# A mixture-of-experts item of 96 token slots instead of 128

## The chip, the core and the metric

One core of a Trainium2 chip runs the whole program. The metric is the device time of one execution in microseconds (us); lower is better. The engines are TensorE (PE; its weight loads, LDWEIGHTS, are listed apart as PEld), VectorE (DVE), ScalarE (ACT), GpSimd (POOL) and the queue engine SyncE (SP).

## The reference, cut to what matters

A decoder trunk of two layers on 256 tokens of 1024 values. Each layer mixes (attention and a recurrence), runs a feed-forward part and adds a gated embedding term. In the second layer the feed-forward part is a mixture of experts:

```
logits = jnp.dot(t, w_router)                        # 256 x 8
top_logit, top_idx = lax.top_k(logits, 2)
top_w = softmax(top_logit)
gate = einsum('tk,tke->te', top_w, one_hot(top_idx, 8))
for e in range(8):
    out = out + gate[:, e:e+1] * ((silu(t @ w_gate[e]) * (t @ w_up[e])) @ w_down[e])
```

Each token goes to two of eight experts, 512 choices in all. An expert's inner width is 3584. All data is 4-byte floating point.

## The kernel before, in words

The work on an expert is an *item*. An item holds up to P = 128 token slots of one expert; if an expert was chosen by more than 128 tokens, a further item is added for the rest (at most OVER of them). The number of items is computed on the chip (`n_items`), and every engine runs a loop over the items.

For an item the 128 tokens are gathered from memory into `xg` (an indirect DMA on POOL, line 529), turned by eight transposes (`turn_tokens`, line 2073) and split into a high and a low part (`uTeh` by ScalarE in `tokens_hi`, line 826; `uTel` by VectorE in `tokens_lo`, line 1419). These are the stationary operands. The weights are the moving operands: they come in chunks of 1 MB (128 x 2048) into a ring `raw` of seven, are split by ScalarE (`whi`, line 599) and VectorE (`wlo`, line 948), and are multiplied in three products (`product`, lines 1601 to 1603: high by high, high by low, low by high), each with 512 moving columns. An item takes 42 chunks in the order `EXP_ORDER`: for each of seven column blocks r of 512 the gate ("g", two halves), the up projection ("u", two halves), and the down projection ("d", two halves) of an earlier block. A gate or up chunk has 4 triples of products, a down chunk 4 as well: 168 triples, 504 products.

The result of a gate block goes through silu (`exs`, line 876), is multiplied with the up block (`exh`, line 1515 on VectorE), is turned by four transposes (`turn`, line 2100), and split again into high (`turn_hi`, line 740, ScalarE) and low (`turn_lo`, line 1500, VectorE); these are the stationary operands of the down products. Each engine works strictly in program order. TensorE issues the four transposes of block r-1 behind the first half of the gate chunk of block r. A transpose has the data as stationary operand and the identity as moving operand. At the end of an item ScalarE copies the 128 x 1024 result out of PSUM (`ysb`, line 840) and POOL scatters its rows (line 553). The last item's result isn't scattered but added by eight products (line 2148).

The slot table: each token's rank within its expert is known from `before` and `ones` products (lines 2052 to 2058). `sel` is a one-hot matrix (token by slot). The first item's tokens are selected by products with it (line 2082, the tokens stationary, `sel` moving; each product is two passes), those of later items by gathers, whose row numbers come from `rows_of_item` (line 2064, `sel` stationary, two moving columns). While item 0 runs, VectorE builds between its splits the table of the items (`table_piece`, one piece per chunk): from chunk OVER_AT = 14 on one overflow column per chunk (`over_item`, lines 1440 to 1443), and behind them one small operation and the list of experts (lines 1458, 1459). Ahead of the loop TensorE also runs transposes that keep it busy (`warm`, line 2031).

Of the kernel before, what the change touches and what calls it, by code (L numbers as in the profile page):

```python
# [41 lines left out]
OVER = (2 * SEQ) // (P + 1)  # L42
# [102 lines left out]
def trunk(nc, x, p, w_in, fox_gate_bias, fox_out_gain, hgrn_lb_logits, hgrn_out_gain, w_out,  # L145
# [3 lines left out]
    with ctx:  # L149
# [94 lines left out]
        exs = [region(512 * i, NC) for i in range(2)]  # L244
        exh = [region(1024 + 512 * i, NC) for i in range(2)]
# [7 lines left out]
        uTeh, uTel = uTh[:, :, 0:P], uTl[:, :, 0:P]  # L253
        exhT = [[hTr[:, i, r * NC:(r + 1) * NC].rearrange("p (c n) -> p c n", c=4) for i in range(2)] for r in range(2)]
# [35 lines left out]
        tprod = small[:, heads_at:heads_at + FIELDS * NE].rearrange("p (a b) -> p a b", a=FIELDS)  # L290
        items = stat(FIELDS * (ITEMS + 1)).rearrange("p (a b) -> p a b", a=FIELDS)
        over, nover, hot = stat(NE), stat(NE), stat(NE)
# [177 lines left out]
        def _(pool):  # L470
# [76 lines left out]
            with pool.Fori(0, last_item) as i:  # L547
# [5 lines left out]
                nc.gpsimd.indirect_dma_start(ybuf, bass.IndirectOffsetOnAxis(ap=put_row, axis=0), ysb, None).then_inc(scattered, 16)  # L553
# [3 lines left out]
        def _(act):  # L557
# [277 lines left out]
            def y_out(i):  # L835
# [3 lines left out]
                for q in range(2):  # L839
                    nc.scalar.activation(ysb[:, q * NC:(q + 1) * NC], bank(5 + q), ACT.Copy).then_inc(y_ready, 1)  # L840
# [27 lines left out]
            def item(i, ahead):  # L868

                for n, (kind, r, hf) in enumerate(EXP_ORDER):  # L870
# [56 lines left out]
        def _(dve):  # L927
# [94 lines left out]
            def rows_to_get(i, b):  # L1022

                dve.wait_ge(row_ps, i + 1)
                link_row(V.tensor_copy(gate_next, bank(b)[:, 1:2]), 8 * i + 1)
                link_row(V.tensor_copy(row_sb, bank(b)[:, 0:1]), 8 * i + 2)
                link_row(V.tensor_scalar(get_row, row_sb, 2.0, -2.0, ALU.max, ALU.add), 8 * i + 3)
                V.tensor_scalar(get_row, get_row, 1, None, ALU.logical_shift_right).then_inc(get_ready, 1)

            def rows_to_put(i):  # L1030

                link_row(V.tensor_scalar(unused, row_sb, 0.0, None, ALU.is_equal), 8 * i + 4)
                link_row(V.tensor_tensor(unused, unused, spare, ALU.mult), 8 * i + 5)
                link_row(V.tensor_copy(tokf[:, 0:1], get_row), 8 * i + 6)
                link_row(V.tensor_copy(gate_of, gate_next), 8 * i + 7)
                dve.wait_ge(scattered, i * 16 + 16)
                V.scalar_tensor_tensor(put_row, row_sb, -2.0, unused, ALU.add, ALU.add).then_inc(put_ready, 1)
# [6 lines left out]
            def choose_slots():  # L1044

                for t in range(TT):
                    V.tensor_scalar(sel[:, t, :], iota[:, :], iitem[:, t:t + 1], None, ALU.is_equal).then_inc(sel_ready, 1)
# [360 lines left out]
            for t in range(TT):  # L1408
                V.tensor_scalar(sel[:, t, :], iota[:, :], table[:, t, 0:1], None, ALU.is_equal).then_inc(sel_ready, 1)
            link(V.tensor_scalar(over, bank(RANKS)[:, 2 * NE:3 * NE], float(P), None, ALU.is_gt))  # L1410
            link(V.tensor_tensor_scan(nover, ones[:, 0:NE], over, 0.0, ALU.mult, ALU.add))
            for k in range(2):
                V.tensor_scalar(item_expert[:, ITEMS + k:ITEMS + k + 1], nover[:, NE - 1:NE], float(NE - k), None, ALU.add).then_inc(count_ready, 1)
            V.tensor_copy(iitem[:, 0:4], table[:, 0:4, 0]).then_inc(first_rows, 1)

            def tokens_lo(i, q):

                dve.wait_ge(euh_ready, i * 2 + (q + 1))
                V.tensor_tensor(uTel[:, 4 * q:4 * q + 4, :], bank(TOKENS[q], 4, P), uTeh[:, 4 * q:4 * q + 4, :].bitcast(F32),
# [18 lines left out]
            def over_item(n):  # L1438

                link(V.tensor_scalar(hot, nover, float(n + 1), None, ALU.is_equal))  # L1440
                link(V.tensor_tensor(hot, hot, over, ALU.mult))
                link(V.tensor_tensor(tprod, table, hot.unsqueeze(1).to_broadcast([P, FIELDS, NE]), ALU.mult))
                link(V.tensor_reduce(items[:, :, NE + n], tprod, AX, ALU.add))

            def table_piece(n):
# [11 lines left out]
                elif n == OVER_AT + OVER:  # L1457
                    link(V.tensor_scalar(items[:, 0:2, NE:ITEMS], items[:, 0:2, NE:ITEMS], -float(P), None, ALU.add))
# [14 lines left out]
            def last_slots():  # L1473

                link(V.tensor_scalar(tokf[:, 1:2], tokf[:, 0:1], -float(P), None, ALU.add))
                for t in range(TT):
                    V.tensor_scalar(slot_of[:, t, :], iota[:, :], tokf[:, t:t + 1], gate_of, ALU.is_equal, ALU.mult).then_inc(slot_ready, 1)
# [735 lines left out]
```

## Time and profile before

| | |
|---|---|
| median of 3 runs | 1541.87 us (1541.39 to 1544.29) |
| profiled execution, span from first to last instruction | 1540.0 us, 21230 instructions |
| what lies around the span (median less span) | 1.87 us |
| busy: PE, PEld, DVE, ACT, POOL | 1518.3, 1281.1, 1231.6, 996.5, 53.9 us |
| mean granted clock of TensorE | 0.997 of 2.4 GHz |
| DMA | 453.38 MB, mean 294 GB/s |
| loads of each of the three expert weights | x112, 1024 KB each (8 items x 14) |

The profile is of one execution; its own device time isn't listed apart from the span, so a change is worked out on the span and then put on the median. Matmuls are pipelined: the recorded time of one is from its start to its modelled end and is longer than the distance to the next one's start. A group like "x8" in a timeline has the time from the first start to the last end.

### The profile page before, as it was taken

The page shows a single profiled execution, that of the slowest core. Times are in us where ns is not written, and L with a number is a line of the kernel's source. Part 1 is how long each engine was busy: PE and PEld are TensorE (multiplying, and loading weights), DVE is VectorE, ACT ScalarE, POOL GpSimd, SP SyncE. Part 2 cuts the span into 40 slices and gives each one's busy share as a digit, 9 for nine tenths or more (in the row PEclk, how much of TensorE's full clock was granted, in tenths as well). Part 3 has the DMA queues.
Part 4 walks back from the last instruction along what each step waited for, and adds up shares of the span by engine and source line. Part 5 has one row for each costly group of instructions (what it writes and reads, how often), then busy time and mean ns, then how long its engine had stood idle before and what let it go on. Part 6 is the DMA issues. An engine that isn't in the chain of part 4 may idle for free.

```text
span 1540.0 us, 21230 instructions
## 1 busy us (share of the span) xinstructions
PE 1518.3 (99%) x7976; PEld 1281.1 (83%) x7976; DVE 1231.6 (80%) x1100; ACT 996.5 (65%) x852; POOL 53.9 (4%) x76
## 2 busy tenths in 40 slices
PE   7999999999999999999999999999999999999998
PEld 6988888888998888888888888888888888888876
DVE  5877545557786679988889889888988889898887
ACT  6544444346725367787787687687787787777666
POOL 5000000000000000000000000000000000000000
PEclk9999999999999999999999999999999999999999
DMA  9432765545533479999999999999999999999990
GB/s 304 138 110 83 256 202 186 188 168 183 165 110 123 172 278 363 383 372 377 378 374 386 378 371 387 373 374 388 374 375 391 370 373 393 369 375 390 373 391 30
DMA packets 206787, 453.38 MB, mean 294 GB/s; under 512 B 12488, under 2 KB 31504, under 8 KB 206480
## 3 DMA queue, kind: packets, MB, share of 16 engines
q1 hardware_dynamic: 200368, 439.22, 79.2%
q0 software_dynamic: 2880, 10.49, 1.8%
q10 hardware_dynamic: 3488, 2.99, 0.6%
q8 instruction: 33, 0.54, 0.1%
q14 instruction: 18, 0.15, 0.0%
HBM read 444.80 MB, written 7.86 MB: 294 GB/s over the span
## 4 chain that ended last, share of the span: by engine, by line
PE 94%; DVE 3%; ACT 1%; DMA 1%; issue 1%; SPq 0%; DVEq 0%; ACTq 0%
PE bank L1601 28%; PE bank L1603 28%; PE bank L1602 28%; PE bank L1692 2%; PE bank L2100 2%; DVE wlo L948 1%; PE bank L1799 1%; PE bank L1752 1%; PE bank L1596 1%; ACT whi L599 0%; DMA raw<-in_w_exp_gate_dram 0%; DMA raw<-in_w_in_dram 0%; PE bank L1766 0%; PE bank L2073 0%; PE bank L1701 0%
## 5 line engine op out<-in xcount | busy, mean ns | idle before, releaser
L948 DVE TENSOR_TENSOR wlo<-raw,whi 128x2048 fp32r<-128x2048 f32 x415 | 937.1, 2288 | 144.5 <-ACT whi L599 92.8
L599 ACT ACTIVATE whi<-raw 128x2048 fp32r<-128x2048 f32 x341 | 638.1, 1911 | 45.5 <-DMA raw<-in_w_exp_down_dram 22.9
L1601 PE MATMUL bank<-whi,uTh 128*128 128x512 f32 (+1 forms) x1304 | 512.0, 393 | 0.9 <-DVE uTl L1014 0.5
L1603 PE MATMUL bank<-whi,uTl 128*128 128x512 f32 (+1 forms) x1304 | 503.8, 386 | 0.0
L1602 PE MATMUL bank<-wlo,uTh 128*128 128x512 f32 (+1 forms) x1304 | 502.8, 386 | 0.0
L1603 PEld LDWEIGHTS bank<-whi,uTl 128*128 128x128 f32 x1304 | 244.9, 188 | 50.6
L1601 PEld LDWEIGHTS bank<-whi,uTh 128*128 128x128 f32 x1304 | 245.1, 188 | 49.1 <-DVE uTl L1014 0.7
L1602 PEld LDWEIGHTS bank<-wlo,uTh 128*128 128x128 f32 x1304 | 245.3, 188 | 46.8
L1601 PE MATMUL bank<-whi,hTr 128*128 128x512 f32 x528 | 207.3, 393 | 0.4 <-DVE hTr L1500 0.4
L1603 PE MATMUL bank<-whi,hTr 128*128 128x512 f32 x528 | 205.7, 390 | 0.0
L1602 PE MATMUL bank<-wlo,hTr 128*128 128x512 f32 x528 | 205.5, 389 | 0.0
L591 ACT ACTIVATE whi<-raw 128x2048 fp32r<-128x2048 f32 x74 | 138.8, 1912 | 0.9 <-DMA raw<-in_w_in_dram 0.8
L740 ACT ACTIVATE hTr<-bank 128x512 fp32r<-128x512 f32 x56 | 33.6, 599 | 153.2 <-PE bank L2100 153.2
L1603 PEld LDWEIGHTS bank<-whi,hTr 128*128 128x128 f32 x528 | 99.1, 188 | 20.9
L1601 PEld LDWEIGHTS bank<-whi,hTr 128*128 128x128 f32 x528 | 99.2, 188 | 20.7 <-issue 0.8
L1602 PEld LDWEIGHTS bank<-wlo,hTr 128*128 128x128 f32 x528 | 99.2, 188 | 20.1
L1601 PE MATMUL bank<-uTh,whi 128*128 128x256 f32 x256 | 74.1, 290 | 0.0
L1602 PE MATMUL bank<-uTl,whi 128*128 128x256 f32 x256 | 72.4, 283 | 0.0
L1603 PE MATMUL bank<-uTh,wlo 128*128 128x256 f32 x256 | 72.4, 283 | 0.0
L783 ACT ACTIVATE hTr<-bank 128x512 fp32r<-128x512 f32 x10 | 5.4, 595 | 74.2 <-PE bank L1955 74.2
L649 ACT ACTIVATE work<-bank 128x512 f32<-128x512 f32 x24 | 14.3, 597 | 57.0 <-PE bank L1603 54.1
L1601 PEld LDWEIGHTS bank<-uTh,whi 128*128 128x128 f32 x256 | 49.1, 192 | 1.2
(294 smaller groups left out, 1086.8 us busy)
## 6 DMA issues: line engine op xcount, KB each, us to landing
raw<-in_w_exp_gate_dram SPq DMA_DIRECT2D x112, 1024.0 KB, 6.0
raw<-in_w_exp_up_dram SPq DMA_DIRECT2D x112, 1024.0 KB, 6.2
raw<-in_w_exp_down_dram SPq DMA_DIRECT2D x112, 1024.0 KB, 6.1
raw<-in_w_in_dram SPq DMA_DIRECT2D x28, 1024.0 KB, 5.4
raw<-in_w_ffn_gate_dram SPq DMA_DIRECT2D x11, 1024.0 KB, 5.3
raw<-in_w_ffn_up_dram SPq DMA_DIRECT2D x11, 1024.0 KB, 5.1
raw<-in_w_ffn_down_dram SPq DMA_DIRECT2D x11, 1024.0 KB, 4.8
raw<-in_w_out_dram SPq DMA_DIRECT2D x8, 1024.0 KB, 5.1
```

Source lines behind the costliest of these rows:

```text
L591: nc.scalar.activation(whi[:, n % SPLIT, :], raw[:, n % RAW, :], ACT.Copy).then_inc(hi_a, 1)
L599: nc.scalar.activation(whi[:, s % SPLIT, :], raw[:, s % RAW, :], ACT.Copy).then_inc(hi_a, 1)
L740: nc.scalar.activation(exhT[r % 2][0], bank(4, 4, P), ACT.Copy).then_inc(exT_hi, 1)
L948: return V.tensor_tensor(wlo[:, n % RAW, :], raw[:, n % RAW, :], whi[:, n % SPLIT, :].bitcast(F32), ALU.subtract).then_inc(lo_ready, 1)
L1596: last = T.transpose(bank(4 + 2 * t + q, 4, P)[:, c, :], un[:, t, (4 * q + c) * P:(4 * q + c + 1) * P], ident[:, :])
L1601: T.matmul(o, sth, mvh, start=start, stop=False)
L1602: T.matmul(o, sth, mvl, start=False, stop=False)
L1603: return T.matmul(o, stl, mvh, start=False, stop=stop)
L1692: last = T.matmul(b[:, t * NP + hp, :], keyT[r, hp, t * P:(t + 1) * P], later, start=True, stop=True)
L1752: last = T.matmul(bank(FOX_BANK[t])[:, hd * HD:(hd + 1) * HD], probsT[u][:, i * nk + kt, :], fv[:, kt, hd * HD:(hd + 1) * HD], start=kt == ...
L1799: last = T.matmul(bank(b[t]), st[:, hf * HALF + k, t * P:(t + 1) * P], mv[:, k, :], start=start and k == 0, stop=stop and k == HALF - 1)
L2100: last = T.transpose(bank(4, 4, P)[:, c, :], exh[r % 2][:, c * P:(c + 1) * P], ident[:, :])
```

## The change

CAP = 96 replaces P = 128 as the number of slots of an item. `uTeh`, `uTel` and `exhT` are 96 columns wide, so that the stationary operands of the products, the PSUM rows that they write, `exs`, `exh` and `ysb` have 96 rows. Transposes read 96 rows and have a 96 x 96 identity. Gather and scatter move 96 rows. An expert of more than 96 tokens gets a second item and one of more than 192 a third; so at most five items are added instead of three (OVER), `over` has two comparisons (96, 192) side by side, and `over_item` works on 2 x 8 columns. The moving operands of the products keep 512 columns, and the loads of weights stay as they are.

```diff
-OVER = (2 * SEQ) // (P + 1)
+CAP = 96
+MORE = (SEQ - 1) // CAP
+OVER = (2 * SEQ) // (CAP + 1)
...
-        exs = [region(512 * i, NC) for i in range(2)]
-        exh = [region(1024 + 512 * i, NC) for i in range(2)]
+        exs = [region(512 * i, NC)[0:CAP, :] for i in range(2)]
+        exh = [region(1024 + 512 * i, NC)[0:CAP, :] for i in range(2)]
...
-        uTeh, uTel = uTh[:, :, 0:P], uTl[:, :, 0:P]
-        exhT = [[hTr[:, i, r * NC:(r + 1) * NC].rearrange("p (c n) -> p c n", c=4) for i in range(2)] for r in range(2)]
+        uTeh, uTel = uTh[:, :, 0:CAP], uTl[:, :, 0:CAP]
+        exhT = [[hTr[:, i, r * NC:r * NC + 4 * CAP].rearrange("p (c n) -> p c n", c=4) for i in range(2)] for r in range(2)]
...
-                nc.gpsimd.indirect_dma_start(xg, None, tok, bass.IndirectOffsetOnAxis(ap=get_row, axis=0)).then_inc(xg_in, 16)
+                nc.gpsimd.indirect_dma_start(xg[0:CAP, :], None, tok, bass.IndirectOffsetOnAxis(ap=get_row[0:CAP, :], axis=0)).then_inc(xg_in, 16)
...
-                nc.scalar.activation(exhT[r % 2][0], bank(4, 4, P), ACT.Copy).then_inc(exT_hi, 1)
+                nc.scalar.activation(exhT[r % 2][0], bank(4, 4, CAP), ACT.Copy).then_inc(exT_hi, 1)
...
-                nc.scalar.activation(uTeh[:, 4 * q:4 * q + 4, :], bank(TOKENS[q], 4, P), ACT.Copy).then_inc(euh_ready, 1)
+                nc.scalar.activation(uTeh[:, 4 * q:4 * q + 4, :], bank(TOKENS[q], 4, CAP), ACT.Copy).then_inc(euh_ready, 1)
...
-                V.tensor_scalar(sel[:, t, :], iota[:, :], table[:, t, 0:1], None, ALU.is_equal).then_inc(sel_ready, 1)
-            link(V.tensor_scalar(over, bank(RANKS)[:, 2 * NE:3 * NE], float(P), None, ALU.is_gt))
-            link(V.tensor_tensor_scan(nover, ones[:, 0:NE], over, 0.0, ALU.mult, ALU.add))
+                V.tensor_scalar(sel[:, t, 0:CAP], iota[:, 0:CAP], table[:, t, 0:1], None, ALU.is_equal).then_inc(sel_ready, 1)
+            for k in range(MORE):
+                V.tensor_scalar(over[:, k * NE:(k + 1) * NE], bank(RANKS)[:, 2 * NE:3 * NE], float((k + 1) * CAP), None, ALU.is_gt).then_inc(dchain, 1)
...
+            link(V.tensor_tensor_scan(nover, ones[:, 0:MORE * NE], over, 0.0, ALU.mult, ALU.add))
...
-                link(V.tensor_scalar(hot, nover, float(n + 1), None, ALU.is_equal))
-                link(V.tensor_tensor(hot, hot, over, ALU.mult))
-                link(V.tensor_tensor(tprod, table, hot.unsqueeze(1).to_broadcast([P, FIELDS, NE]), ALU.mult))
-                link(V.tensor_reduce(items[:, :, NE + n], tprod, AX, ALU.add))
+                link(V.scalar_tensor_tensor(hot, nover, float(n + 1), over, ALU.is_equal, ALU.mult))
+                link(V.tensor_reduce(above[:, n:n + 1], hot[:, NE:MORE * NE], AX, ALU.add))
+                hots = hot.rearrange("p (m b) -> p m b", m=MORE).unsqueeze(1).to_broadcast([P, FIELDS, MORE, NE])
+                link(V.tensor_tensor(tprod, table.unsqueeze(2).to_broadcast([P, FIELDS, MORE, NE]), hots, ALU.mult))
+                link(V.tensor_reduce(items[:, :, NE + n], tprod.rearrange("p a m b -> p a (m b)"), AX, ALU.add))
...
-                V.tensor_tensor(exh[r % 2], bank(2 + r % 2), exs[r % 2], ALU.mult).then_inc(exh_ready, 1)
+                V.tensor_tensor(exh[r % 2], bank(2 + r % 2)[0:CAP, :], exs[r % 2], ALU.mult).then_inc(exh_ready, 1)
...
-                        last = T.transpose(bank(TOKENS[q], 4, P)[:, c, :], xg[:, k * P:(k + 1) * P], ident[:, :])
+                        last = T.transpose(bank(TOKENS[q], 4, CAP)[:, c, :], xg[0:CAP, k * P:(k + 1) * P], ident[0:CAP, 0:CAP])
...
-                        last = T.matmul(bank(TOKENS[q], 4, P)[:, c, :], un[:, t, k * P:(k + 1) * P], sel[:, t, :], start=t == 0, stop=t == TT - 1)
+                        last = T.matmul(bank(TOKENS[q], 4, CAP)[:, c, :], un[:, t, k * P:(k + 1) * P], sel[:, t, 0:CAP], start=t == 0, stop=t == TT - 1)
...
-                        last = T.transpose(bank(4, 4, P)[:, c, :], exh[r % 2][:, c * P:(c + 1) * P], ident[:, :])
+                        last = T.transpose(bank(4, 4, CAP)[:, c, :], exh[r % 2][:, c * P:(c + 1) * P], ident[0:CAP, 0:CAP])
...
-                            last = product(bank(5 + q), exhT[r % 2][0][:, cc, :], exhT[r % 2][1][:, cc, :], wh[:, c, s], wl[:, c, s],
+                            last = product(bank(5 + q)[0:CAP, :], exhT[r % 2][0][:, cc, :], exhT[r % 2][1][:, cc, :], wh[:, c, s], wl[:, c, s],
...
-                            last = product(bank((0 if kind == "g" else 2) + r % 2), uTeh[:, kk, :], uTel[:, kk, :],
+                            last = product(bank((0 if kind == "g" else 2) + r % 2)[0:CAP, :], uTeh[:, kk, :], uTel[:, kk, :],
```

## Rows read from the trace of the kernel before

**Rows 1.** Page, part 1: busy time, share of the span, instructions.
```profile
PE 1518.3 (99%) x7976; PEld 1281.1 (83%) x7976; DVE 1231.6 (80%) x1100; ACT 996.5 (65%) x852; POOL 53.9 (4%) x76
```

**Rows 2.** Page, part 4: the chain that ended last, by engine.
```profile
PE 94%; DVE 3%; ACT 1%; DMA 1%; issue 1%; SPq 0%; DVEq 0%; ACTq 0%
```

**Rows 3.** Windows: length; busy PE, PEld, DVE, ACT, POOL; granted clock, DMA share, GB/s.
```profile
536.00:537.00 1.00, 1.00 (x6) 1.00 (x5) 0.90 (x6) 0.00 (x0) 0.00 (x0) 0.50 0.00 0
...
700.00:800.00 100.00, 100.00 (x459) 82.79 (x458) 88.63 (x57) 76.11 (x53) 4.08 (x4) 1.00 1.02 374
```

**Rows 4.** The gather's line: ns min/median/max, first and last start.
```profile
L529 POOL DMA_INDIRECT work<-tok,small x8: 961/962/1017, 625.9 to 1459.9; - x8
```

**Rows 5.** Groups by line and shape: busy us, mean ns, idle before, by whom.
```profile
L1601 PE MATMUL bank<-whi,hTr 128*128 128x512 f32 x528 | 207.3, 393 | 0.4 <-DVE hTr L1500 0.4
...
L1500 DVE TENSOR_TENSOR hTr<-bank,hTr 128x512 fp32r<-128x512 f32 x56 | 38.5, 688 | 9.1 <-ACT hTr L740 9.0
...
L2100 PE MATMUL bank<-ident,work 128*128 128x128 f32 x224 | 33.6, 272 | 0.8 <-DVE work L1515 0.8
```

**Rows 6.** Timeline of TensorE in the expert loop: start us, us.
```profile
900.65 0.39 PE L1601 MATMUL bank<-whi,hTr 128*128 128x512 f32 x1
900.65 0.19 PEld L1602 LDWEIGHTS bank<-wlo,hTr 128*128 128x128 f32 x1
...
903.37 0.39 PE L1601 MATMUL bank<-whi,uTh 128*128 128x512 f32 x1
```

**Rows 7.** Timeline in layer 0, 256 moving columns, then 64-row operands.
```profile
62.49 0.28 PE L1602 MATMUL bank<-uTl,whi 128*128 128x256 f32 x1
...
62.61 0.28 PE L1603 MATMUL bank<-uTh,wlo 128*128 128x256 f32 x1
62.82 0.97 PEld L1692 LDWEIGHTS bank<-work 64*128 64x128 f32 x16
```

**Rows 8.** Timeline: eight transposes of an item's tokens.
```profile
652.20 1.03 PE L2073 MATMUL bank<-ident,work 128*128 128x128 f32 x8
```

**Rows 9.** Single lines of TensorE: duration ns min/median/max, first and last start.
```profile
L2040 PEld LDWEIGHTS bank<-wr,work x32: 186/192/192, 523.6 to 532.1; 128*128 128x128 f32 x32
L2040 PE MATMUL bank<-wr,work x32: 175/256/277, 523.7 to 532.2; 128*128 128x8 f32 x32
...
L2073 PEld LDWEIGHTS bank<-ident,work x64: 138/140/141, 652.0 to 1486.9; 128*128 128x128 f32 x64
...
L2148 PE MATMUL bank<-work x8: 592/592/697, 1499.5 to 1502.6; 128*128 128x512 f32 x8
```

**Rows 10.** Timeline ahead of the expert loop.
```profile
523.70 1.85 PE L2040 MATMUL bank<-wr,work 128*128 128x8 f32 x16
...
537.44 5.20 PE L2082 MATMUL bank<-work,un 128*128 128x128 f32 x32
540.89 0.60 ACT L826 ACTIVATE uTh<-bank 128x512 fp32r<-128x512 f32 x1 [5.62 <-PE bank L2082]
```

**Rows 11.** Timeline of VectorE in item 0, chunks 14 to 21.
```profile
590.27 0.17 DVE L1440 TENSOR_SCALAR small<-small 128x8 f32<-128x8 f32 x1
...
590.67 0.22 DVE L1442 TENSOR_TENSOR small<-small 128x56 f32<-128x56 f32 x1
...
591.17 0.69 DVE L1515 TENSOR_TENSOR work<-bank,work 128x512 f32<-128x512 f32 x1
...
594.88 0.69 DVE L1500 TENSOR_TENSOR hTr<-bank,hTr 128x512 fp32r<-128x512 f32 x1
...
598.78 2.29 DVE L948 TENSOR_TENSOR wlo<-raw,whi 128x2048 fp32r<-128x2048 f32 x1 [0.23 <-DVE small L1443]
...
607.88 0.68 DVE L1515 TENSOR_TENSOR work<-bank,work 128x512 f32<-128x512 f32 x1
```

**Rows 12.** Timeline of TensorE in the same stretch.
```profile
595.70 0.49 PE L1601 MATMUL bank<-whi,hTr 128*128 128x512 f32 x1 [0.37 <-DVE hTr L1500]
...
609.43 0.60 PE L2100 MATMUL bank<-ident,work 128*128 128x128 f32 x4
```

More of the change, by code:

```diff
@@ L289, in trunk @@
         table = stat(FIELDS * NE).rearrange("p (a b) -> p a b", a=FIELDS)
-        tprod = small[:, heads_at:heads_at + FIELDS * NE].rearrange("p (a b) -> p a b", a=FIELDS)
+        tprod = small[:, heads_at:heads_at + FIELDS * MORE * NE].rearrange("p (a m b) -> p a m b", a=FIELDS, m=MORE)
         items = stat(FIELDS * (ITEMS + 1)).rearrange("p (a b) -> p a b", a=FIELDS)
-        over, nover, hot = stat(NE), stat(NE), stat(NE)
+        over, nover, hot, above = stat(MORE * NE), stat(MORE * NE), stat(MORE * NE), stat(OVER)
         iitem = stat(6)
@@ L552, in _ @@
                 nc.gpsimd.tensor_tensor(idle, spare, spare, ALU.add).then_inc(pool_turn, 1)
-                nc.gpsimd.indirect_dma_start(ybuf, bass.IndirectOffsetOnAxis(ap=put_row, axis=0), ysb, None).then_inc(scattered, 16)
+                nc.gpsimd.indirect_dma_start(ybuf, bass.IndirectOffsetOnAxis(ap=put_row[0:CAP, :], axis=0), ysb[0:CAP, :], None).then_inc(scattered, 16)
             fetch(n_items, n_items * 2)
@@ L1024, in rows_to_get @@
                 dve.wait_ge(row_ps, i + 1)
[L1025 to L1028, printed above, removed]
+                link_row(V.tensor_copy(gate_next[0:CAP, :], bank(b)[0:CAP, 1:2]), 8 * i + 1)
+                link_row(V.tensor_copy(row_sb[0:CAP, :], bank(b)[0:CAP, 0:1]), 8 * i + 2)
+                link_row(V.tensor_scalar(get_row[0:CAP, :], row_sb[0:CAP, :], 2.0, -2.0, ALU.max, ALU.add), 8 * i + 3)
+                V.tensor_scalar(get_row[0:CAP, :], get_row[0:CAP, :], 1, None, ALU.logical_shift_right).then_inc(get_ready, 1)
             def rows_to_put(i):
[L1032 to L1035, printed above, removed]
+                link_row(V.tensor_scalar(unused[0:CAP, :], row_sb[0:CAP, :], 0.0, None, ALU.is_equal), 8 * i + 4)
+                link_row(V.tensor_tensor(unused[0:CAP, :], unused[0:CAP, :], spare[0:CAP, :], ALU.mult), 8 * i + 5)
+                link_row(V.tensor_copy(tokf[0:CAP, 0:1], get_row[0:CAP, :]), 8 * i + 6)
+                link_row(V.tensor_copy(gate_of[0:CAP, :], gate_next[0:CAP, :]), 8 * i + 7)
                 dve.wait_ge(scattered, i * 16 + 16)
-                V.scalar_tensor_tensor(put_row, row_sb, -2.0, unused, ALU.add, ALU.add).then_inc(put_ready, 1)
+                V.scalar_tensor_tensor(put_row[0:CAP, :], row_sb[0:CAP, :], -2.0, unused[0:CAP, :], ALU.add, ALU.add).then_inc(put_ready, 1)
             def link_row(ins, n):
@@ L1046, in choose_slots @@
                 for t in range(TT):
-                    V.tensor_scalar(sel[:, t, :], iota[:, :], iitem[:, t:t + 1], None, ALU.is_equal).then_inc(sel_ready, 1)
+                    V.tensor_scalar(sel[:, t, 0:CAP], iota[:, 0:CAP], iitem[:, t:t + 1], None, ALU.is_equal).then_inc(sel_ready, 1)
             def choose(t):
@@ L1408, in _ @@
             for t in range(TT):
[L1409 to L1411 removed]
+                V.tensor_scalar(sel[:, t, 0:CAP], iota[:, 0:CAP], table[:, t, 0:1], None, ALU.is_equal).then_inc(sel_ready, 1)
+            for k in range(MORE):
+                V.tensor_scalar(over[:, k * NE:(k + 1) * NE], bank(RANKS)[:, 2 * NE:3 * NE], float((k + 1) * CAP), None, ALU.is_gt).then_inc(dchain, 1)
+            chain[0] += MORE
+            dve.wait_ge(dchain, chain[0])
+            link(V.tensor_tensor_scan(nover, ones[:, 0:MORE * NE], over, 0.0, ALU.mult, ALU.add))
             for k in range(2):
[L1413 removed]
+                V.tensor_scalar(item_expert[:, ITEMS + k:ITEMS + k + 1], nover[:, MORE * NE - 1:MORE * NE], float(NE - k), None, ALU.add).then_inc(count_ready, 1)
             V.tensor_copy(iitem[:, 0:4], table[:, 0:4, 0]).then_inc(first_rows, 1)
@@ L1457, in table_piece @@
                 elif n == OVER_AT + OVER:
-                    link(V.tensor_scalar(items[:, 0:2, NE:ITEMS], items[:, 0:2, NE:ITEMS], -float(P), None, ALU.add))
+                    ranks_over = items[:, 0:2, NE:ITEMS]
+                    link(V.scalar_tensor_tensor(ranks_over, above.unsqueeze(1).to_broadcast([P, 2, OVER]), -float(CAP), ranks_over, ALU.mult, ALU.add))
+                    link(V.tensor_scalar(ranks_over, ranks_over, -float(CAP), None, ALU.add))
                     V.tensor_copy(item_expert[:, 0:ITEMS], items[:, FIELDS - 1, 0:ITEMS]).then_inc(table_ready, 1)
@@ L1473, in last_slots @@
             def last_slots():
-                link(V.tensor_scalar(tokf[:, 1:2], tokf[:, 0:1], -float(P), None, ALU.add))
+                link(V.tensor_scalar(tokf[0:CAP, 1:2], tokf[0:CAP, 0:1], -float(P), None, ALU.add))
                 for t in range(TT):
-                    V.tensor_scalar(slot_of[:, t, :], iota[:, :], tokf[:, t:t + 1], gate_of, ALU.is_equal, ALU.mult).then_inc(slot_ready, 1)
+                    V.tensor_scalar(slot_of[0:CAP, t, :], iota[0:CAP, :], tokf[0:CAP, t:t + 1], gate_of[0:CAP, :], ALU.is_equal, ALU.mult).then_inc(slot_ready, 1)
             def add_last(t):
@@ L2063, in rows_of_item @@
                 for t in range(TT):
-                    last = T.matmul(bank(b)[:, 0:2], sel[:, t, :], iitem[:, 2 + t:5 + t:2], start=t == 0, stop=t == TT - 1)
+                    last = T.matmul(bank(b)[0:CAP, 0:2], sel[:, t, 0:CAP], iitem[:, 2 + t:5 + t:2], start=t == 0, stop=t == TT - 1)
                 last.then_inc(row_ps, 1)
@@ L2147, in _ @@
                         pe.wait_ge(y_ready, n_items * 2 + (1 + q))
-                    T.matmul(bank(LAST_BANK[t][q]), slot_of[:, t, :], ysb[:, q * NC:(q + 1) * NC], start=True, stop=True).then_inc(last_y, 1)
+                    T.matmul(bank(LAST_BANK[t][q]), slot_of[0:CAP, t, :], ysb[0:CAP, q * NC:(q + 1) * NC], start=True, stop=True).then_inc(last_y, 1)
             embed(1, tail_in(0), 0)
```

10 lines of the change are left out of this document (5 added, 5 removed).

## The prediction

> **What bounds the kernel now.** I read the page first, then the windows, then single stretches of the timeline. TensorE is busy for 99% of the span [rows 1], and the chain that ended last is 94% TensorE [rows 2]. The view by windows repeats this for the expert loop: in 700 to 800 us TensorE is busy for 100.00 of 100 us at the full granted clock (2.4 GHz), VectorE for 88.63, ScalarE for 76.11 [rows 3]. The gather for the next item starts first at 625.9 and last at 1459.9 us, eight times [rows 4], so an item takes (1459.9 - 625.9)/7 = 119.1 us and eight of them some 950 of the 1540 us.
>
> Busy time says nothing of pace, so I looked at starts. Two products of line 1601 stand twelve products apart at 900.65 and 903.37 [rows 6]: one starts every 2.72/12 = 0.2267 us, though each is recorded as 0.39 us. With 256 moving columns the starts are 0.120 apart [rows 7]. So a moving column costs (226.7 - 120)/256 = 0.417 ns and 13.3 ns remain per product, with either width. The weight load (0.19 us) starts with the product before it and lies under it. An item has 168 triples, 504 products: 504 x 0.2267 = 114.3 us. Its 36 transposes start (1.03 - 0.272)/7 = 0.108 us apart [rows 5, 8]: 3.9 us. Together 118.2 of 119.1. The item's time is therefore set by moving columns and transposes; what lies on other engines is free as long as TensorE does not wait.
>
> **The change part by part.** The reference's router, evaluated on its inputs, gives the eight experts 66, 65, 55, 64, 45, 82, 67 and 68 of the 512 choices. None passes 96, so no overflow item is added and there stay eight items. If one were, it would cost 119.1 us.
>
> (1) *The 4032 expert products.* The moving side stays 512 columns; only the stationary side goes from 128 to 96 columns. What could answer to that is the remainder of 13.3 ns. No row has a stationary side under 128 columns. If the remainder were in proportion to the width it would fall by 3.3 ns, 13.5 us in all; if it were to vanish, 54 us; if it grew by as much as the first, +13.5. I take 0: transposes swap 128 columns of weights just as often and show only 108 - 107 = 1 to 2 ns (below), so the 13.3 ns do not come from swapping a wide operand. The shorter weight load is hidden under 0.2267 us of the product before it; it has 0.04 us to grow before it shows.
>
> (2) *The transposes.* The data is the stationary operand and keeps 128 columns; the identity is the moving one and goes from 128 to 96. A moving column of this 4-byte kind costs (592 - 272)/384 = 0.833 ns (512 columns in line 2148, 128 in line 2100) [rows 5, 9], so 128 cost 106.7 ns: the whole interval of 108 but 1 to 2 ns. Then 96 cost 80, and an interval falls by 26.7 ns, provided that the weight load isn't the limit. Bounds: 0 if it is, 26.7 if not. The router's products (line 2040) tell what the limit of a load is: with only 8 moving columns they start (1.85 - 0.256)/15 = 0.106 us apart [rows 9, 10], so a load that is recorded as 192 ns takes the array for 0.106. A transpose's load is recorded as 140 ns, 52 shorter [rows 9]; if the fixed part is the same it takes the array for 0.054. That is under 80, and I take the gain. It holds between transposes only: the product behind the last one needs a load of the long kind (0.106), as now. Seven groups of four give 3 intervals each, the group of eight gives 7: 28 x 26.7 = 0.75 us per item, x8 = -6.0 us.
>
> The Trainium skill ("TensorE: Matmul & The Clock Gate", LDWEIGHTS) has a load take its column count over 1.2 GHz, which is 107 ns for 128 columns, transposes not excepted. By it every transpose would stay at 107 and this term would be 0. The interval of line 2040 agrees with it, the 140 ns of the transposes' loads speak against it.
>
> (3) *The row products (line 2064)*: four per item, 2 moving columns, so bound by their load; 96 columns instead of 128 at 0.106/128 per column take 26 ns less each. 4 x 0.026 x 8 = -0.8 us; bounds 0 and -0.8. I take -0.8.
>
> (4) *Ahead of the loop*: the 32 passes that select the first item's tokens (line 2082) get 96 moving columns. Until 540.89 they start (540.89 - 537.44)/16 = 0.216 us apart, twice 0.106, at the lower clock (granted 0.50, 1.2 GHz) [rows 3, 10]; their load keeps 128 columns, so I take 0 (bound: 16 x 0.053 = -0.85). Behind them lie one ScalarE and one VectorE operation on 384 instead of 512 columns: 0.60 and 0.69 us for 512 [rows 5, 10], some 0.1 us less each: -0.2. The two comparisons and the longer scan on VectorE come before 540 us, while TensorE is in line 2082: nothing.
>
> (5) *The table in item 0.* VectorE now makes five overflow columns and not three, between the weight splits. One costs 591.17 - 590.27 = 0.90 us now [rows 11]. With 112 elements for 56 in the product and the reduction (0.22 against 0.17 for 8 elements: 0.05 per 48, so 0.06 more each) and 16 for 8 elsewhere I take 1.08. VectorE is already late there: line 1515 at 591.17 and line 1500 at 594.88 follow without a gap, and TensorE idles before the product behind (0.37) [rows 11, 12]. The first two columns lie in this stretch: 2 x 0.18 - 0.13 (line 1500 is shorter) = +0.23. From there to line 1515 at 607.88 come one longer column, two new ones and one more small operation: 0.18 + 2.16 + 0.2 = 2.54. VectorE has 0.23 idle (598.78), and line 1515 ends at 608.56 while TensorE wants it at 609.43 [rows 12]: 0.8 of slack after the hand-over. 2.54 - 0.23 - 0.8 = +1.5. Later gaps absorb the rest. Together +1.7; bounds +0.2 (ScalarE, not VectorE, was late) and +2.9 (all that is added shows).
>
> (6) *Hidden*: lines 740 and 1500 lose some 0.1 us in each of 56 turns, silu and the gate product keep their 512 columns, the gathers and scatters move a quarter fewer rows. TensorE waited 0.4 us for line 1500 in the whole kernel [rows 5] and for no gather, so this gives nothing; without that cover it would be some 0.2 us per turn, 56 times, -11.
>
> Sum: 0 - 6.0 - 0.8 - 0.2 + 1.7 = -5.3 us on a span of 1540.0. The span plus 1.87 us is the median of the runs shown; the time is thus 1541.87 - 5.3 = 1536.6 us (-0.34%).
>
> **The rivals.**
> *Loads bind the transposes* (the change does not do what it could): term 2 falls away. 1541.87 - 1.0 + 1.7 = 1542.6, no change. For it: 0.108 is also next to the 0.106 of a load. Against: the record of 140 ns.
> *The remainder follows the width*: 4032 x 3.3 ns = 13.5 us more gain, 1523; the same upwards, 1550. For it: nothing in the trace fixes the remainder. Against: it is the same for 256 and 512 moving columns and absent in transposes.
> *A drain at every change of shape* (slower). When the stationary rows go from 128 to 64, the load isn't pulled ahead: it starts at 62.82, 0.21 after the product at 62.61, where the next load otherwise starts with the product, and that product's interval is 0.12 [rows 7]; the next start comes 0.2 us late. After the change transposes are 96 rows by 128 columns and products 128 by 96, and they alternate 16 times per item. 16 x 8 x 0.2 = +25.6, so 1562. It decides (over +3.1 us net) from (3.1 + 5.3)/128 = 0.066 us per switch. Against: transposes and products of one shape are all that the loop shows.
> The Trainium skill ("TensorEngine Tiling (Array Packing)", Key Properties and Column Tiling) says that a change of tiling mode drains the engine, with modes for up to 64 rows or columns; 96 would be the full mode, and by it nothing drains. The switch at 62.61 agrees; no run here shows 96.
> *An overflow item*: 1661, excluded by the counts.
>
> **How the numbers follow.** Forecast 0.52; loads bind 0.18; remainder smaller 0.12, larger 0.09; drain 0.08; overflow 0.01. What a measurement of this kernel tells from no change is about 0.2%, 3.1 us. The forecast's own range is 1534 (the item-0 term hidden but for 0.2, and a little less in term 2) to 1540 (half of term 2, all of term 5); 0.07 of its 0.52 lie within 0.2%. Faster: 0.45 + 0.12 = 0.57. Same: 0.07 + 0.16. Slower: 0.09 + 0.08 + 0.01 + 0.02. The range goes from 1523 (remainder in proportion) to 1547 (loads bind, all of term 5, and half a nanosecond more per product).
>
> **What the profile after would show.** Starts of expert products still 0.2267 apart; the eight transposes of line 2073 in 0.83 instead of 1.03 us and their duration 245 instead of 272 ns; an item 0.8 us shorter, 118.3; in item 0 a wait of TensorE for line 1515 of some 1.5 us; DMA issues still x112 per weight. The prediction is wrong if the product interval moves by a nanosecond (4 us), if the load of a transpose shows as the limit, or if a load is no longer pulled ahead at a switch.

## The result, and the profile after

The changed kernel takes 1546.93 us (median of 6 runs, 1544.68 to 1549.13), the kernel before on the same chip 1542.32 us (6 runs, 1540.97 to 1544.53). The ratio is 1.0027 [1.0017, 1.0037]: 4.6 us slower, where 1536.6 us (5.3 us faster) was forecast. Line numbers have moved on by two to eight: the products are now lines 1609 to 1611, the transposes 2108 (block) and 2081 (tokens), the gather 531, VectorE's gate product 1523 and its low half 1508.

The page of the kernel after, busy time, chain and one DMA line:

```profile
PE 1524.4 (99%) x7976; PEld 1170.2 (76%) x7976; DVE 1223.1 (79%) x1110; ACT 987.0 (64%) x852; POOL 74.2 (5%) x76
...
PE 94%; DVE 3%; DMA 1%; ACT 1%; issue 0%; SPq 0%; DVEq 0%; ACTq 0%
...
raw<-in_w_exp_gate_dram SPq DMA_DIRECT2D x112, 1024.0 KB, 5.6
```

Beside [rows 1, 2] all is as announced but one thing: weight loads, VectorE and ScalarE have less to do, no item was added (x112), TensorE is still 94% of the chain, and yet its busy time rose by 6.1 us with the same 7976 instructions. The window in the loop, with the columns of [rows 3]:

```profile
700.00:800.00 100.00, 100.00 (x457) 70.66 (x456) 86.38 (x56) 75.91 (x54) 6.14 (x4) 1.00 1.02 372
```

TensorE is as full as before, at the same full granted clock, and starts 457 instructions where it started 459. It isn't waiting more; its instructions start further apart. The timeline of TensorE, for [rows 6]:

```profile
902.12 0.39 PE L1609 MATMUL bank<-whi,hTr 128*96 128x512 f32 x1
902.12 0.16 PEld L1610 LDWEIGHTS bank<-wlo,hTr 128*96 128x96 f32 x1
...
904.89 0.39 PE L1609 MATMUL bank<-whi,hTr 128*96 128x512 f32 x1
```

These starts too are twelve products apart: 2.77/12 = 0.2308 us, against 0.2267. The load fell from 0.19 to 0.16 us and still starts with the product ahead of it. The recorded duration shows next to none of this (0.39 us in both, 389 and 392 ns in the median of lone products further down): only starts do. A timeline rounds to 10 ns, so I also took the mean distance of neighbouring products in 680 to 1480 us: 227.3 ns over 3268 pairs before, 230.3 ns over 3252 after, +3.0.

The transposes, for [rows 4, 8, 9], views by timeline and by source line:

```profile
656.73 0.82 PE L2081 MATMUL bank<-ident,work 96*128 96x96 f32 x8
...
L2081 PEld LDWEIGHTS bank<-ident,work x64: 138/140/143, 656.5 to 1494.4; 96*128 96x128 f32 x64
L2081 PE MATMUL bank<-ident,work x64: 243/246/248, 656.7 to 1494.5; 96*128 96x96 f32 x64
...
L531 POOL DMA_INDIRECT work<-tok,small x8: 970/3290/3304, 632.8 to 1467.3; - x8
```

Eight in 0.82 us of 246 ns each: starts (0.82 - 0.246)/7 = 0.082 apart, as forecast (0.83 in all, 245 each). The loads of this line give the time of an item, (1494.4 - 656.5)/7 = 119.70 us, against (1486.9 - 652.0)/7 = 119.27 before [rows 9]: +0.43 where -0.8 was expected.

Around one turn of a block in the loop, kernel after:

```profile
716.20 0.40 PE L1611 MATMUL bank<-whi,uTl 128*96 128x512 f32 x1
716.44 0.49 PE L2108 MATMUL bank<-ident,work 96*128 96x96 f32 x4
716.72 0.45 PE L1609 MATMUL bank<-whi,uTh 128*96 128x512 f32 x1
717.01 0.39 PE L1610 MATMUL bank<-wlo,uTh 128*96 128x512 f32 x1
```

From the first transpose to the second product 0.57 us pass; before it was 0.68 (712.50 to 713.18 in its trace), and over the 47 turns in 680 to 1480 us the means are 0.565 and 0.669. For one item: 504 x 3.0 ns = +1.51; seven turns at -0.104 = -0.73; the tokens' turn -0.21; the row products -0.12. Together +0.45, where +0.43 was measured; the measured one times eight is +3.4 us.

Item 0, where VectorE makes five columns and not three (kernel after, VectorE then TensorE):

```profile
593.27 0.17 DVE L1445 SCALAR_TENSOR_TENSOR small<-small 128x16 f32<-128x16 f32 x1
594.29 0.69 DVE L1523 TENSOR_TENSOR work<-bank,work 96x512 f32<-96x512 f32 x1
...
613.15 0.68 DVE L1523 TENSOR_TENSOR work<-bank,work 96x512 f32<-96x512 f32 x1
```

```profile
612.47 0.40 PE L1611 MATMUL bank<-whi,uTl 128*96 128x512 f32 x1
613.89 0.55 PE L2108 MATMUL bank<-ident,work 96*128 96x96 f32 x4 [1.02 <-DVE work L1523]
```

A column costs 594.29 - 593.27 = 1.02 us (0.90 before, 1.08 forecast). TensorE starts the transposes of block 3 at 613.89, 1.42 us after the product ahead instead of 0.23: a stall of 1.19 us.

So +3.4 for eight items, +1.2 for item 0, and -0.3 from line 2063 to the first expert product (9.99 us against 10.27): +4.3 of the +4.6. The profiled execution was the longest of its kernel (span 1547.3, +7.3 on before). Of the rest of that, 1.7 us lie ahead of the first product of line 1700 (64.6 us after the start, before 62.8; two experiments built on the changed kernel have 64.2 and 62.5, and one built on the kernel before has 64.0) and 1.4 us between lines 1916 and 2063 ahead of the loop, where the clock stood at half for longer: at 0.50 from 533.3 to 543.5 us, against 533.7 to 540.5 in before. The same stretch took 10.5 us in before and in all seven experiments on whole kernels, so neither belongs to the change.

### The profile page after: what moved, and what is told of

It is laid out like the page before. It is cut to its first block, busy times and chain, and to the rows that moved or that the text cites. A ratio compares the mean times of both kernels' runs of the same rounds, so it can differ in the third digit from the quotient of the medians.

```text
span 1547.3 us, 21242 instructions
## 1 busy us (share of the span) xinstructions
PE 1524.4 (99%) x7976; PEld 1170.2 (76%) x7976; DVE 1223.1 (79%) x1110; ACT 987.0 (64%) x852; POOL 74.2 (5%) x76
## 4 chain that ended last, share of the span: by engine, by line
PE 94%; DVE 3%; DMA 1%; ACT 1%; issue 0%; SPq 0%; DVEq 0%; ACTq 0%
PE bank L1609 28%; PE bank L1611 28%; PE bank L1610 28%; PE bank L1700 2%; DVE wlo L950 2%; PE bank L2108 1%; PE bank L1807 1%; PE bank L1760 1%; DMA raw<-in_w_exp_up_dram 1%; PE bank L1604 1%; DMA raw<-in_w_in_dram 0%; PE bank L1774 0%; PE bank L1709 0%; PE bank L1734 0%; PE bank L2081 0%
## 5 line engine op out<-in xcount | busy, mean ns | idle before, releaser
L1609 PE MATMUL bank<-whi,uTh 128*96 128x512 f32 (+2 forms) x1304 | 511.8, 392 | 0.8 <-DVE uTl L1016 0.6
L1611 PE MATMUL bank<-whi,uTl 128*96 128x512 f32 (+2 forms) x1304 | 505.2, 387 | 0.0
L1610 PE MATMUL bank<-wlo,uTh 128*96 128x512 f32 (+2 forms) x1304 | 504.7, 387 | 0.0
L1611 PEld LDWEIGHTS bank<-whi,uTl 128*96 128x96 f32 (+1 forms) x1304 | 221.2, 170 | 76.2
L1609 PEld LDWEIGHTS bank<-whi,uTh 128*96 128x96 f32 (+1 forms) x1304 | 221.4, 170 | 73.4 <-DVE uTl L1016 0.7
L1610 PEld LDWEIGHTS bank<-wlo,uTh 128*96 128x96 f32 (+1 forms) x1304 | 221.6, 170 | 70.8
L1609 PE MATMUL bank<-whi,hTr 128*96 128x512 f32 (+1 forms) x528 | 208.5, 395 | 0.5 <-DVE hTr L1508 0.5
L1611 PE MATMUL bank<-whi,hTr 128*96 128x512 f32 (+1 forms) x528 | 207.1, 392 | 0.0
L1610 PE MATMUL bank<-wlo,hTr 128*96 128x512 f32 (+1 forms) x528 | 206.6, 391 | 0.0
L1611 PEld LDWEIGHTS bank<-whi,hTr 128*96 128x96 f32 (+1 forms) x528 | 87.2, 165 | 34.6
L1609 PEld LDWEIGHTS bank<-whi,hTr 128*96 128x96 f32 (+1 forms) x528 | 87.2, 165 | 33.6 <-issue 0.9
L1610 PEld LDWEIGHTS bank<-wlo,hTr 128*96 128x96 f32 (+1 forms) x528 | 87.4, 166 | 33.1
```

The lines of the kernel that those rows point to most:

```text
L1609: T.matmul(o, sth, mvh, start=start, stop=False)
L1610: T.matmul(o, sth, mvl, start=False, stop=False)
L1611: return T.matmul(o, stl, mvh, start=False, stop=stop)
```

## The experiments

Each ratio is to the kernel before on the same chip. Product intervals are the mean over neighbouring products in 680 to 1480 us. "After" or "before" says which kernel an edit starts from.

### Products 128 wide again, all else as after

```diff
-        uTeh, uTel = uTh[:, :, 0:CAP], uTl[:, :, 0:CAP]
+        uTeh, uTel = uTh[:, :, 0:P], uTl[:, :, 0:P]
-        exhT = [[hTr[:, i, r * NC:r * NC + 4 * CAP].rearrange(...) for i in range(2)] for r in range(2)]
+        exhT = [[hTr[:, i, r * NC:(r + 1) * NC].rearrange(...) for i in range(2)] for r in range(2)]
...
-   last = T.transpose(bank(4, 4, CAP)[:, c, :], exh[r % 2][...], ident[0:CAP, 0:CAP])
+   last = T.transpose(bank(4, 4, P)[:, c, 0:CAP], exh[r % 2][...], ident[0:CAP, 0:CAP])
...
-   last = product(bank(5 + q)[0:CAP, :], exhT[r % 2][0][:, cc, :], ...)
+   last = product(bank(5 + q), exhT[r % 2][0][:, cc, :], ...)
```

> The changed kernel, but the expert products have 128 stationary columns again (gate, up and down; 128 output rows); transposes, gathers, the slot table and the item count stay as changed. The columns from 96 on hold whatever lay there, no slot uses them. The two ScalarE and VectorE splits of a turn are 512 wide again. Theory A (the product itself gets slower with 96 stationary columns): starts back to 227.0 ns apart, 4032 x 3.2 = 13 us less than the changed kernel, so some 1534 us, 0.5% under the kernel before. Theory B (something around the products, the narrower loads of transposes or the other engines' new rhythm, stretches them): starts stay at 230 ns and the time at 1546.

Measured: 1536.74 us (1535.3 to 1539.72), ratio 0.9971 [0.996, 0.9981]; product interval 227.3 ns.

```profile
900.26 0.39 PE L1609 MATMUL bank<-whi,hTr 128*128 128x512 f32 x1
...
902.98 0.39 PE L1609 MATMUL bank<-whi,hTr 128*128 128x512 f32 x1
...
L2081 PEld LDWEIGHTS bank<-ident,work x64: 138/140/143, 654.3 to 1483.2; 96*128 96x128 f32 x64
```

The starts, twelve products apart, are 2.72 us from each other, as in [rows 6]. An item takes (1483.2 - 654.3)/7 = 118.41 us, 0.86 less than before. With the products' width back, the rest of the change gains what the forecast had for it. The whole miss is in the products.

### Before, with only the products 96 wide

```diff
-   last = product(bank(5 + q), exhT[r % 2][0][:, cc, :], exhT[r % 2][1][:, cc, :], ...)
+   last = product(bank(5 + q)[0:96, :], exhT[r % 2][0][:, cc, 0:96], exhT[r % 2][1][:, cc, 0:96], ...)
...
-   last = product(bank(...), uTeh[:, kk, :], uTel[:, kk, :], ...)
+   last = product(bank(...)[0:96, :], uTeh[:, kk, 0:96], uTel[:, kk, 0:96], ...)
```

> The kernel before, with one edit: the expert products use 96 of the 128 stationary columns and write 96 output rows; all else is 128 wide. Slots from 96 on are not computed (none is filled). Theory A: starts 230.3 ns apart, +13 us, 1555 us, slower than both kernels. Theory B: 227 ns and 1542 us.

Measured: 1551.58 us (1551.52 to 1554.0), ratio 1.0071 [1.0057, 1.0085]; interval 230.0 ns. The timeline of TensorE:

```profile
713.04 0.60 PE L2100 MATMUL bank<-ident,work 128*128 128x128 f32 x4
713.40 0.48 PE L1601 MATMUL bank<-whi,uTh 128*96 128x512 f32 x1
713.72 0.39 PE L1602 MATMUL bank<-wlo,uTh 128*96 128x512 f32 x1
...
905.90 0.39 PE L1601 MATMUL bank<-whi,uTh 128*96 128x512 f32 x1
...
908.66 0.39 PE L1601 MATMUL bank<-whi,uTh 128*96 128x512 f32 x1
```

Twelve products in 2.76 us, and the turn of a block still 0.68 us. 4032 x 2.7 ns = 10.9 us; by the ratio it is 1542 x 0.0071 = 10.9. The data behind the operands, their places and all other work were those of before: the width alone does it.

### After, with three overflow columns

```diff
-OVER = (2 * SEQ) // (CAP + 1)
+OVER = (2 * SEQ) // (P + 1)
```

> The changed kernel with three overflow columns in the table instead of five (a table for at most three extra items, as before; no input here needs any). Takes two of the pieces of 0.99 us out of VectorE's item 0. If the wait of TensorE in item 0 (1.19 us at the turn of block 3) comes from them, it vanishes and the time falls by some 1.2 us (1545.7), else nothing changes.

Measured: 1543.41 us (1542.87 to 1546.2), ratio 1.0015 [1.0006, 1.0024]. From the first block's transposes to item 1's tokens pass 94.5 us against 95.7 after: 1.2 us, the stall seen above. The intervals of the ratios just overlap, but the trace names the place.

### Products by themselves at several widths

No part of the reference is left: rows of 60 products of one width, behind each other on TensorE.

```diff
+for j in range(REPS):
+    T.matmul(b[0:M, 0:N], st[0:K, j % 16, c0:c0 + M], mv[0:K, j % 4, 0:N], ...)
```

> A kernel of its own, nothing of the reference: rows of 60 back-to-back products on resident data, with no DMA and no other engine at work, for stationary widths of 128, 120, 112, 104, 97, 96, 88, 80, 65, 64 and 32 columns, 96 columns from column 32 on, 96 rows by 128 and by 96, with 256 moving columns, and in the two-pass 4-byte form. Theory A: 227.0 ns at 128 and 230.3 at 96 columns here too. If the interval depends on a multiple of 32 or on the load's length, the other widths show which. Theory B: no difference between widths, and perhaps 215 ns throughout, since no other engine reads memory.

Each row gives (time - duration of one)/59:

```profile
24.15 14.22 PE L77 MATMUL bank<-mv,st 128*120 128x512 f32 x60
...
205.58 7.45 PE L77 MATMUL bank<-mv,st 128*128 128x256 f32 x60
...
212.89 7.20 PE L77 MATMUL bank<-mv,st 128*96 128x256 f32 x60
...
323.15 13.89 PE L77 MATMUL bank<-mv,st 128*128 128x512 f32 x60
...
336.90 14.03 PE L77 MATMUL bank<-mv,st 128*96 128x512 f32 x60
```

With 512 moving columns: 128 wide 228.8 ns, 120 234.3, 112 230.1, 104 230.0, 97 234.1, 96 231.1, 88 234.2, 80 233.8, 65 235.1, 64 230.5, 32 231.8. With 256 the sign turns round: 121.4 for 128, 117.3 for 96. So the cost shows without whi, wlo, VectorE or any DMA beside it, isn't in proportion to the width, and is no property of 96: of these widths, none is faster than 128. With 96 rows instead of 128 the intervals are the same (228.5 and 231.2). The first distance of a row is longer than the rest (0.31 us behind a product 128 wide); without it the means are 227.4 ns for 128 and 230.0 for 96, just those of the kernels. As two-pass products, the widths take 429.8 and 429.6 ns for each pass (120 records for 60 products).

### Before, with the products 120 wide

The edit is that of the second experiment with 0:120 for 0:96.

> The kernel before with the expert products 120 columns wide instead of 128 (slots from 120 on are not computed; none is filled). The row of lone products gave starts 234.3 ns apart at 120 columns against 228.8 at 128. If the width alone sets the interval in the kernel too: starts 5 ns further apart than before, some 232.5 ns, and 1562 us. If 96 is special, or the interval is in proportion to the columns left out: under 1 ns more, 1545 us at most.

Measured: 1565.38 us (2 runs, 1564.29 to 1566.46), ratio 1.0148 [1.0125, 1.017]; interval 233.3 ns.

```profile
903.13 0.40 PE L1601 MATMUL bank<-whi,hTr 128*120 128x512 f32 x1
...
905.94 0.40 PE L1601 MATMUL bank<-whi,hTr 128*120 128x512 f32 x1
```

A cut of eight columns costs 23 us: 4032 x 6.0 ns = 24. The lone products' order of 128, 96 and 120 holds in the kernel.

### Lone products with fewer moving columns, and moved in their tile

No part of the reference is left here either. Rows of 100 products; M columns from column `so` of the stationary tile, N from `mo` of the moving one.

> Lone products again, rows of 100: 128 and 96 stationary columns at 512, 480, 448, 384, 320 and 256 moving columns, then with the first stationary column at 8, 16, 32, 64 and the first moving column at 8, 32. If a narrow operand costs something fixed per product, 96 stays 2 to 3 ns above 128 at every moving width. If it is how the load's reads fall into the running product (a collision in memory), the difference depends on the moving width and on the addresses, and may change sign (the first such kernel had 117.3 for 96 and 121.4 for 128 at 256 moving columns).

```profile
275.63 23.49 PE L78 MATMUL bank<-mv,st 128*128 128x512 f32 x100
...
298.98 22.94 PE L78 MATMUL bank<-mv,st 128*128 128x512 f32 x100
...
344.80 23.05 PE L78 MATMUL bank<-mv,st 128*96 128x512 f32 x100
...
507.52 22.92 PE L78 MATMUL bank<-mv,st 128*128 128x512 f32 x100
...
530.30 23.23 PE L78 MATMUL bank<-mv,st 128*96 128x512 f32 x100
```

The last two are plain: 227.6 and 230.7 ns. The first is 128 wide from column 32: 233.3; the second from column 64: 227.8; the third 96 wide from column 16: 228.9. A move of the operand, with the same shape, is worth up to 6.5 ns (column 16: 234.1), more than the step from 128 to 96 columns. Between 480 and 320 moving columns neither width wins by more than 1.3 ns (217.7 and 219.0; 147.4 and 147.2), except at 448: 207.4 and 203.3.

### The move in the kernel: before from column 32, after from column 16

```diff
-        uTeh, uTel = uTh[:, :, 0:P], uTl[:, :, 0:P]
+        uTeh, uTel = uTh[:, :, 32:32 + P], uTl[:, :, 32:32 + P]
```
```diff
-        uTeh, uTel = uTh[:, :, 0:CAP], uTl[:, :, 0:CAP]
+        uTeh, uTel = uTh[:, :, 16:16 + CAP], uTl[:, :, 16:16 + CAP]
```

> The kernel before with one edit: the tokens' stationary operands (gate and up products, 2688 of the 4032) lie 32 columns (128 bytes) further on; width 128, nothing else changes. Theory A (the number of stationary columns sets the interval): 227 ns and 1542 us, no change. Theory C (the addresses that a load reads while the product before it streams set it; width is one way to change them): the lone products gave 233.3 ns for this offset, so 6 ns x 2688 = +16 us, 1558 us, and down products unchanged at 227.

> The changed kernel with the tokens' stationary operands 16 columns (64 bytes) further on, still 96 wide. Theory A: 1546 us, no change. Theory C: the lone products gave 228.9 instead of 230.7 ns for this offset at 96 columns, so -1.8 x 2688 = -5 us, 1541 us.

Measured, before moved: 1555.39 us (1554.67 to 1556.27), ratio 1.0084 [1.0068, 1.0101]. Its timeline, a down product first and then the tokens' products:

```profile
907.06 0.40 PE L1603 MATMUL bank<-whi,hTr 128*128 128x512 f32 x1
907.30 0.40 PE L1601 MATMUL bank<-whi,uTh 128*128 128x512 f32 x1
...
910.09 0.39 PE L1601 MATMUL bank<-whi,uTh 128*128 128x512 f32 x1
```

Tokens' products start 2.79/12 = 0.2325 us apart; the down products, whose operand wasn't moved, have 227.9 ns in the same trace (227.0 before). 13.2 us are lost without one column fewer, by the first column alone.

Measured, after moved: 1542.24 us (1540.86 to 1544.82), ratio 0.9999 [0.9989, 1.001].

```profile
905.68 0.39 PE L1609 MATMUL bank<-whi,uTh 128*96 128x512 f32 x1
...
908.42 0.39 PE L1609 MATMUL bank<-whi,uTh 128*96 128x512 f32 x1
```

2.74/12 = 0.2283; the mean over 680 to 1480 us is 228.7, where the changed kernel has 230.0, and the down products remain near 231. By the ratios, moving two thirds of the operands by 16 columns takes back the whole loss. The intervals account for 2688 x 1.3 ns = 3.4 us of it; the rest is within what the ratios can tell.

### More addresses

No part of the reference is left. Rows of 100 lone products again.

> Lone products, rows of 100, 512 moving columns: with one or eight stationary tiles and one or three moving tiles, widths of 64, 32 and 8 columns at offsets of 0, 32 and 64 columns, 128 columns at offsets 1, 4, 128 and with both operands moved by 32, 96 columns at 24, 48, 112 at 0 and 16, 120 at 8, and the same in 2-byte type. Theory C: intervals go by where a load starts and ends against 64 columns (256 bytes): 128 wide at offset 128 is as fast as at 0, at 1 and 4 as slow as at 8 (234), 112 at 16 and 120 at 8 (ends at 128) differ from 112 and 120 at 0; which tile is read makes no difference. Theory A: only the width counts and offsets were chance.

```profile
265.27 23.49 PE L83 MATMUL bank<-mv,st 128*128 128x512 f32 x100
...
288.63 22.92 PE L83 MATMUL bank<-mv,st 128*128 128x512 f32 x100
...
311.42 22.94 PE L83 MATMUL bank<-mv,st 128*128 128x512 f32 x100
...
496.11 22.93 PE L83 MATMUL bank<-mv,st 128*120 128x512 f32 x100
...
519.13 21.53 PE L83 MATMUL bank<-bm,bs 128*128 128x512 bf16 x98
...
540.53 21.76 PE L83 MATMUL bank<-bm,bs 128*96 128x512 bf16 x100
```

The first three are 128 wide, from column 1, from column 4, and with both operands from column 32. From column 1: 233.3 ns. From column 4: 227.6, where I had expected it as slow as 8 (234.1 in the run before). Stationary from 32 and moving from 32 together: 227.8, though either alone gives 233. 120 wide from column 8: 227.7, against 234.3 from column 0. One stationary tile or eight, one moving tile or three: 227.8 (128 wide) and 230.7 (96) throughout. 96 wide from 48 gives 234.0, from 24 231.1; stationary from 16 with moving from 32 gives 233.8. 112 wide goes the other way from 120: 229.8 from column 0, 232.3 from 16. So most of the difference isn't width as such, and it isn't which tiles alternate: it follows the columns at which the two operands lie. Something may be left for the width, since no place tried brings 96 under 228.9. The one width under 128 that matched it is 8 columns, 226.8.

As 2-byte products neither width nor place matters: 128 wide from column 0, 128 wide from column 32 and 96 wide all start 215 or 216 ns apart. (Of the two rows 128 wide the trace lacks two records, one of them in the middle, where a distance of 432 ns stands, so they can't be read by dividing by 99.)

### Products 128 wide, overflow columns spread out

On top of the first experiment:

```diff
-OVER_AT = 14
+OVER_CHUNKS = [17, 22, 28, 31, 34]
...
-                elif OVER_AT <= n < OVER_AT + OVER:
-                    over_item(n - OVER_AT)
-                elif n == OVER_AT + OVER:
+                elif n in OVER_CHUNKS:
+                    over_item(OVER_CHUNKS.index(n))
+                elif n == OVER_CHUNKS[-1] + 2:
```

> e1 (96-slot items, products 128 wide) with the five overflow columns spread over item 0: behind chunks 17, 22, 28, 31 and 34 and the list at 36, in place of 14 to 18 and 19. If lateness of VectorE is what holds TensorE at the turns of blocks 2 and 3 (1.2 us and some 0.5 us in the changed kernel), both waits vanish: 1.5 us less than e1, some 1535.2 us. If one piece alone delays a turn wherever it stands, no more than 0.5 us is gained.

Measured: 1535.74 us (1534.65 to 1536.71), ratio 0.9955 [0.994, 0.997]. The view by source line of the blocks' transposes (2108), in 556 to 660 us, lists the engine's idle time before them with reason, us and times; in the kernel after that is 3.0 us in 3 waits, in the first experiment 3.8 in 4 (a wait can stand there twice, for the load and for the product), and here:

```profile
  DVE work L1523: 0.3, 1
```

It is the best version, 6.3 us under before and 11 under after. Over the first experiment it gains 1.0 us by the medians and 2.5 by the ratios, whose intervals overlap; the evidence is in the traces. From the first block's transposes to item 1's tokens pass 92.7 us against 95.4, 2.6 less.

## Why the prediction was wrong

**The step that failed is part (1), the remainder of a product.** The forecast took the 13.3 ns beyond the moving columns as untouched by the width. They are 16.3 with 96 columns: +3.0 x 4032 = +12.1 us (second experiment, products alone: +10.9). The forecast had this as a rival ("the same upwards, 1550") at 0.09, and its own sign of being wrong, a product interval that moves by a nanosecond, is what came. That the rival's +13.5 lies near is luck: it stands for a remainder in proportion to the columns left out, and 120 columns (+6.0 ns) cost twice what 96 do. The argument was that transposes swap as wide an operand and show only 1 to 2 ns. That compares a load against another moving read: the experiments show the remainder to depend on how the two operands lie to each other, which a transpose's rows can't tell. The second argument against the rival, the same remainder at 256 and 512 columns [rows 7], was a coincidence of two points: with 96 wide the change from 128 is +2.3 ns at 512 and -4.1 at 256 (lone products). Nor is the remainder one number with 128 wide: by the same 0.417 ns a column, 480 moving columns leave 17.7 ns and 448 leave 20.7, where 256, 320, 384 and 512 leave 14.

That 1546.93 lies inside the stated range of 1523 to 1547 is luck too. The top was built of a refuted rival, loads that bind, and it is added up too high: 1541.87 - 1.0 + 2.9 + 2.0 = 1545.8.

**Part (2), the transposes: right.** 82 ns apart where 81.3 was forecast (108 - 26.7). The first experiment takes 0.86 us off an item, parts (2) and (3) said 0.85. The rival that loads bind is refuted: the load is recorded as 140 ns as before, and the starts are 82 apart. By the Trainium skill ("TensorE: Matmul & The Clock Gate", LDWEIGHTS) they would have stayed at 107; the trace contradicts it for these loads. A detail was missed: in the changed kernel the interval between the two products behind a block's transposes is 0.29 and not 0.32 us. With only the transposes narrow (first experiment) or only the products (second) it stays at 0.32, so it takes both; why isn't shown.

**Part (3), the row products: right.** In the first experiment the stretch from the first of line 2072 to the second product behind it is 0.60 us, before it was 0.69; forecast 0.10 less. **Part (4)** is right as far as it can be told: the stretch that holds it is 0.3 us shorter, and 0.1 to 0.4 in the four experiments built on the changed kernel, where 0.2 was forecast.

**Part (5), item 0: right in mechanism, somewhat too large.** A column 1.02 for 1.08, the stall in front of block 3 1.19 us for 1.5, named at the right instruction; the third experiment takes 1.2 away again. The +0.23 of the first two columns didn't show: the stalls at block 2 are 0.23 and 0.62 us, before they were 0.35 and 0.53.

**Part (6), hidden work: right.** Line 1508 fell from 688 to 551 ns in 56 turns, VectorE's share of 700 to 800 us by 2.25 us, and TensorE gained nothing by it. Gathers of 96 rows held POOL for 3.0 us instead of 0.97; no engine waited for them.

**The drain: refuted.** The first transpose of a turn starts 0.23 us behind the last product (median of 47 turns; the same before), and the next product 0.28 behind that (0.36 before: three distances of 27 ns more). The Trainium skill ("TensorEngine Tiling (Array Packing)", Key Properties) ties a drain to a change of tiling mode. Its modes end at 64 rows or columns, and the trace shows no drain at 96.

With +12.1 for 0 in part (1), 0.03 us gained behind each of the nine groups of transposes and row products of an item (-2.2 in all), and 1.2 for 1.7 in part (5), the forecast's own sum reads 12.1 - 6.8 - 0.2 - 2.2 + 1.2 = +4.1; measured +4.6.

**What stays open.** Why a position is fast or slow, and why only for 4-byte products. That the load's reads and the moving operand's collide in memory would fit a dependence on both positions together, but no run shows the mechanism. Nor is there a rule for good columns: 0, 4, 64 and 128 are good for 128 wide, 1, 8, 16 and 32 are bad. Other first columns of the down products' operand (`exhT`), which might bring 96 wide to 227 everywhere, weren't tried.

## What to carry to other kernels

When 4-byte products were bound by 512 moving columns, fewer stationary columns saved nothing, and from column 0 on widths of 32 to 120 cost 1 to 3% of each; a move by some columns gave it back for 120 (227.7 from column 8) and in part for 96 (228.9 from column 16). Measure the distance of starts, since a product's recorded duration stays at 0.39 to 0.40 us. A remainder that the trace shows for one width only is an unknown of the size (instructions x remainder), both ways: 4032 x 3 ns outweighed every term that could be read. Here the best version cuts the width where it is on the moving side (the identity of a transpose), and keeps the stationary side at 128, stale columns and all.

## Not expected of the hardware

- The interval of a 4-byte one-pass product with 512 moving columns lies between 226.8 (8 wide) and 235.1 ns (65 wide) with the shape of its stationary operand and the first column of either operand; moving both by 32 columns restores 227.8 (128 wide). A 2-byte product shows none of this: 216 ns in three such rows.
- 96 stationary columns are slower than 128 at 512 moving columns (230.7 against 227.6) and faster at 256 (116.5 against 120.8).
- A gather of 96 rows held POOL 3290 ns in the median (the first of a run took 970) and landed after 8.9 us; one of 128 rows 962 ns and 6.1 us. All five programs with 96 rows and all four with 128 show it.
